# Hybrid decoder trunk on one core: the narrow projections' three products of 256 columns become one of 512 and one of 256

## The chip, the cores and the metric

One core of a Trainium2 chip runs the whole program. The time is device microseconds of one execution of the program, weights and activations being in the chip's own memory at the start.

## The reference

Two layers of one mixer each over 256 tokens of width 2048, then a last RMSNorm. All in float32.

```python
for l in range(DEPTH):
    h = rmsnorm(x, norm_w[l])
    proj = jnp.einsum('bld,dn->bln', h, w_in[l]).astype(f32)
    (gdn_qkv, gdn_b, gdn_a, gdn_z, hg_q, hg_f, hg_i, hg_g, s5_u, s5_z,
     ret_q, ret_k, ret_v, ret_g, gate_logits) = jnp.split(proj, split_idx, axis=-1)
    ...
    ys = jnp.stack([y_a, y_b, y_c, y_d], axis=2).astype(x.dtype)
    branch = jnp.einsum('blcw,cwd->blcd', ys, w_branch[l]).astype(f32)
    merged = jnp.sum(gates * branch, axis=2)
    x = x + jnp.einsum('bld,de->ble', merged.astype(x.dtype), w_out[l])
```

The four branches are a gated DeltaNet (short causal convolution on query, key and value, L2 norms of key and query, chunkwise inverse), HGRN2, an S5 state space scan and a RetNet retention with rotary positions; each has 8 heads or 8 slices of 128 channels.

## The kernel before

A layer has two parts. First come eight **units**, one for each head (u = 0 to 7; n counts them over both layers, 0 to 15). A unit projects h for its 128 channels of all branches and does the mixing of that head in all four branches. Then come the stages behind the units: gates, the GLU of S5, the branch products and the output projection.

**Precision.** Every weight is used as a high part (`w_hi`, the weight as fp32r) and a low part (`w_lo`, the rest), and so is h (`h_hi`, `h_lo`). A product is three passes of PE that add up in one bank: w_hi with h_hi, w_hi with h_lo, w_lo with h_hi (`three_pass`, L1794).

**Slots.** Weights come in slots of 512 KB, four buffers in turn (RING = 4). For each slot SyncE loads `raw_w`, ACT copies it to `w_hi` (`split_hi`, L651), DVE subtracts to get `w_lo` (`split_lo`, L1223), PE multiplies. For slots 6, 8, 10, 16, 18, 20 and 22 of a unit (DMA_LOW) half of the low part is made by ACT (L649) and a DMA of GpSimd, and DVE makes only the other half. A unit has 28 slots:

- 0 to 11 and 20 to 27: the ten **narrow** blocks, two slots each, in the order S5 input (SU), key (GK), query (GQ), forget gate (HF), HGRN query (HQ), value (GV); after the joint slots retention query (RQ), key (RK), gate (RG), and S5 gate (SZ). Weights are the stationary operand, h moves with 256 columns, output is channels by tokens in half a bank. Two banks, PJ[0] and PJ[1], are used in turn.
- 12 to 19: the **joint** slots, h stationary, 512 columns of weights moving, both PJ banks whole.

**Order.** The order on each engine is written out by hand, and every engine works strictly in its own order. `project(i)` on PE waits for the low part of slot i and, at a block's first slot, for `pj_read`, which tells that the bank's last block has been read; its last product counts `split_used`. On ACT and DVE `ahead(i)` makes the high or low part of slot i + 4. DVE's `ahead` waits for ACT's (`hi_ready`), ACT's for PE's end of slot i (`split_used`). Between these stand the steps of the mixing. ACT reads each narrow block out of its bank (`projected(b)` waits for PE's last slot of the block), in the form that it needs: `stage_conv` copies it for the convolution (L766) and scales it by the last tap (L767), `stage_rope` copies it and its swapped halves (L816 to L818), the others are one activation each (L829, L881, L897, L954, L962).

**The chain to the norms.** DVE's `conv_taps` (L1367) adds the other three taps, ACT's `silu_conv` applies SiLU (L776) and squares (L779), and PE's `g_norms`, behind slot 7, sums the squares of key and query (the product with `ones`, bank GB), followed by `g_gram_k` (bank S). DVE then makes the norm factors (`gnorm` L1518, GpSimd's power L585, `gfac` L1524), the masked Gram matrix, and with `invert` and PE's `g_tx`, `g_txt` the inverse level by level; `h_scores` (L1436 on) are the levels of HGRN2. `s5_turn` (L1402 to L1405), `s5_add` (L1411, L1412) and `s5_scan` (L1420) are the state space steps, `ret_finish` (L1344) and `rope` (L1462 to L1465) belong to retention. In the traces the buffers conv_in and gk, gq, gv read partly as mix and work, since names are shared; the rows give the lines.

Of the kernel before, what the change touches and what calls it, by code (L numbers as in the profile page):

```python
# [21 lines left out]
P = 128  # L22
D_MODEL, SEQ, DEPTH = 2048, 256, 2
# [23 lines left out]
(B_SU, B_GK, B_GQ, B_HF, B_HQ, B_GV, B_RQ, B_RK, B_RG, B_SZ) = range(10)  # L47

# [115 lines left out]
def trunk_kernel(nc, A, out):  # L164
# [4 lines left out]
    with ctx:  # L169
# [25 lines left out]
        h_hi, h_lo = sb("h_hi", [P, KT, SEQ], f32r), sb("h_lo", [P, KT, SEQ], f32r)  # L195
# [179 lines left out]
        pj_read = sem("pj_read")  # L375
# [16 lines left out]
        u_staged, s5_used = sem("u_staged"), sem("s5_used")  # L392
# [229 lines left out]
        def _(act):  # L622
# [30 lines left out]
            for l in range(DEPTH):  # L653
# [84 lines left out]
                for u in range(UNITS):  # L738
# [6 lines left out]
                    def projected(b):  # L745

                        act.wait_ge(split_used, s0 + (block_slot(b) + 2 + RING))
                        return PJ[b % 2][:, 0:SEQ]

# [13 lines left out]
                    def stage_conv(b, m):  # L763

                        src = projected(b)
                        A_(conv_in[m][:, CONV - 1:], src, ACT.Copy)  # L766
                        A_((gk, gq, gv)[m], src, ACT.Copy, scale=tap(m, CONV - 1)).then_inc(pj_read, 1)  # L767
# [45 lines left out]
                    def stage_rope(m, b):  # L813

                        src = projected(b)
                        A_(rx[m][:, :], src, ACT.Copy)  # L816
                        A_(rsw[m][0:64, :], src[64:128, :], ACT.Copy)
                        A_(rsw[m][64:128, :], src[0:64, :], ACT.Copy).then_inc(pj_read, 1)  # L818
                        act.drain().then_inc(rope_staged, 1)
# [6 lines left out]
                    def stage_u():  # L826

                        act.wait_ge(s5_used, n1)
                        A_(s_u[:, :], projected(B_SU), ACT.Copy).then_inc(pj_read, 1)  # L829
                        act.drain().then_inc(u_staged, 1)  # L830

                    ahead(0)
                    if u == 0:
                        stage_u()
# [26 lines left out]
                    else:  # L861
                        stage_bc()
                        delta_finish(u - 1)
                        stage_u()
# [16 lines left out]
                    A_(hsig[:, 0, :], projected(B_HF), ACT.Tanh, scale=0.5).then_inc(pj_read, 1)  # L881
# [15 lines left out]
                    A_(hq[:, :], projected(B_HQ), ACT.Silu).then_inc(pj_read, 1)  # L897
# [56 lines left out]
                    A_(gate_of(3), projected(B_RG), ACT.Silu).then_inc(pj_read, 1)  # L954
# [5 lines left out]
                    if u + 1 < UNITS:  # L960
                        cosines()
                    A_(zs[:, ds(u, 1), :].rearrange("p a n -> p (a n)"), projected(B_SZ), ACT.Silu).then_inc(  # L962
                        pj_read, 1)
# [398 lines left out]

# [967 lines left out]
```

## Time and profile before

| | |
|---|---|
| median of three runs | 2917.91 us (2917.57 to 2918.38) |
| the profiled execution | 2917.88 us, its span 2916.0 us |
| granted clock of TensorE, mean | 0.998 |
| PE, DVE, ACT, GpSimd busy | 98%, 68%, 54%, 14% |
| read from memory | 487 MB, 168 GB/s over the span |

The span is that from the first to the last instruction; about 1.9 us lie around it. PE is the matmul side of TensorE. Busy times of PE count products that overlap, so the rate at which it works is read from the starts of its instructions.

### The profile page before, as it was taken

What the parts mean: (1) busy time and instruction counts of PE and PEld (TensorE: products, weight loads), DVE (VectorE), ACT (ScalarE), POOL (GpSimd) and SP (SyncE); (2) the same over time, 40 slices, a digit from 0 to 9 for tenths busy, and PEclk for the clock granted to TensorE, in tenths of its full rate; (3) what the DMA queues carried; (4) which work ended last, traced back from release to release, by engine and by line L of the source; (5) the groups of instructions that cost most, each with busy time, mean ns of one, the idle gap of its engine ahead of it and who ended that gap; (6) DMA issues with size and microseconds to landing.
All of it is one profiled execution on the core that took longest, in us unless ns stands there. A gap on an engine that the chain in (4) does not pass through costs nothing.

```text
span 2916.0 us, 46745 instructions
## 1 busy us (share of the span) xinstructions
PE 2869.0 (98%) x17852; PEld 2562.9 (88%) x17852; DVE 1977.4 (68%) x3177; ACT 1574.0 (54%) x2401; POOL 422.3 (14%) x637
## 2 busy tenths in 40 slices
PE   7999999999999999999999999999999999999998
PEld 6899999999998888888889999999999888888887
DVE  6887788778875555555567877788778755555554
ACT  6556665666564444444556556655665644444443
POOL 3223132213200000000011332123211000000000
PEclk9999999999999999999999999999999999999999
DMA  6676677677766666666656766676667666666655
GB/s 163 163 172 166 175 181 174 164 177 179 175 175 195 194 194 195 193 192 185 192 129 165 178 171 174 172 179 171 171 171 181 181 195 195 192 192 195 194 180 166
DMA packets 636367, 521.56 MB, mean 179 GB/s; under 512 B 26480, under 2 KB 504496, under 8 KB 635760
## 3 DMA queue, kind: packets, MB, share of 16 engines
q1 hardware_dynamic: 612944, 483.46, 59.1%
q0 software_dynamic: 22816, 34.00, 6.8%
q8 instruction: 141, 2.31, 0.3%
q10 hardware_dynamic: 384, 1.11, 0.1%
q14 instruction: 82, 0.67, 0.1%
HBM read 487.02 MB, written 2.10 MB: 168 GB/s over the span
## 4 chain that ended last, share of the span: by engine, by line
PE 65%; issue 26%; DVE 4%; ACT 2%; DVEq 1%; POOL 1%; DMA 1%; ACTq 0%; POOLq 0%
PE PJ L1794 42%; PE S L1794 16%; PE RA L1794 3%; PE GB L1794 2%; DVE mix L1367 1%; DVE w_lo L1223 1%; POOL gnorm L585 0%; POOL w_lo L500 0%; DVE region L1402 0%; ACT w_lo L649 0%; DVE region L1404 0%; DVE region L1405 0%; DVEq L1406 0%; DVE region L1412 0%; DVEq L1413 0%
## 5 line engine op out<-in xcount | busy, mean ns | idle before, releaser
L1223 DVE TENSOR_TENSOR w_lo<-raw_w,w_hi 128x1024 fp32r<-128x1024 f32 (+1 forms) x912 | 1055.3, 1160 | 757.3 <-ACT w_hi L651 729.9
L651 ACT ACTIVATE w_hi<-raw_w 128x1024 fp32r<-128x1024 f32 x912 | 962.5, 1058 | 791.4 <-PE PJ L1794 342.5
L1794 PE MATMUL PJ<-h_hi,w_hi 128*128 128x256 f32 x2560 | 744.7, 291 | 1.6 <-DMA w_lo<-raw_w 1.6
L1794 PE MATMUL PJ<-h_hi,w_lo 128*128 128x256 f32 x2560 | 724.5, 283 | 0.0
L1794 PE MATMUL PJ<-h_lo,w_hi 128*128 128x256 f32 x2560 | 724.3, 283 | 0.0
L1794 PEld LDWEIGHTS PJ<-h_hi,w_hi 128*128 128x128 f32 x2560 | 490.4, 192 | 9.7 <-issue 6.8
L1794 PEld LDWEIGHTS PJ<-h_lo,w_hi 128*128 128x128 f32 x2560 | 490.6, 192 | 0.0
L1794 PEld LDWEIGHTS PJ<-h_hi,w_lo 128*128 128x128 f32 x2560 | 489.9, 191 | 0.0
L1794 PE MATMUL PJ<-w_hi,h_hi 128*128 128x512 f32 x1152 | 461.5, 401 | 1.9 <-DVE h_lo L1698 1.9
L1794 PE MATMUL PJ<-w_hi,h_lo 128*128 128x512 f32 x1152 | 450.4, 391 | 0.0
L1794 PE MATMUL PJ<-w_lo,h_hi 128*128 128x512 f32 x1152 | 449.9, 391 | 0.0
L1794 PEld LDWEIGHTS PJ<-w_hi,h_lo 128*128 128x128 f32 x1152 | 216.7, 188 | 46.6
L1794 PEld LDWEIGHTS PJ<-w_hi,h_hi 128*128 128x128 f32 x1152 | 217.2, 189 | 43.5 <-DVE h_lo L1698 2.4
L1794 PEld LDWEIGHTS PJ<-w_lo,h_hi 128*128 128x128 f32 x1152 | 217.1, 188 | 41.3
L1794 PE MATMUL S<-w_hi,h_hi 128*128 128x512 f32 x576 | 224.6, 390 | 0.0
L1794 PE MATMUL S<-w_hi,h_lo 128*128 128x512 f32 x576 | 224.2, 389 | 0.0
L1794 PE MATMUL S<-w_lo,h_hi 128*128 128x512 f32 x576 | 224.2, 389 | 0.0
L500 POOL DMA_DIRECT2D w_lo<-raw_w x112 | 99.0, 884 | 464.5 <-ACT w_lo L649 448.1
L795 ACT ACTIVATE work<-work 128x128 f32<-128x128 f32 x96 | 30.1, 313 | 201.7 <-PE S L1794 201.7
L1794 PEld LDWEIGHTS S<-w_hi,h_lo 128*128 128x128 f32 x576 | 108.1, 188 | 22.5
L1428 DVE TENSOR_TENSOR region<-region 128x1024 f32<-128x1024 f32 x96 | 117.6, 1225 | 15.1 <-issue 13.6
L1794 PEld LDWEIGHTS S<-w_lo,h_hi 128*128 128x128 f32 x576 | 108.2, 188 | 22.3
(386 smaller groups left out, 3988.6 us busy)
## 6 DMA issues: line engine op xcount, KB each, us to landing
raw_w<-w_in SPq DMA_DIRECT2D x576, 512.0 KB, 3.9
raw_w<-w_in SPq DMA_DIRECT2D x512, 128.0 KB, 2.7
raw_w<-w_branch SPq DMA_DIRECT2D x128, 512.0 KB, 4.2
raw_w<-w_out SPq DMA_DIRECT2D x64, 512.0 KB, 4.1
w_lo<-raw_w POOLq DMA_DIRECT2D x112, 256.0 KB, 4.3
raw_w<-s_glu_w SPq DMA_DIRECT2D x16, 512.0 KB, 4.5
ret_decay<-c_ret POOLq DMA_DIRECT2D x16, 128.0 KB, 3.8
out<-x_tok SPq DMA_DIRECT2D x4, 512.0 KB, 4.0
```

The lines of the kernel that those rows point to most:

```text
L500: pool.dma_start(w_lo[i % RING][:, OWN:, :], raw_w[i % RING][:, OWN:, :], accum_op=ALU.add).then_inc(low_landed, 16)
L651: A_(w_hi[i % RING][:, :, :], raw_w[i % RING][:, :, :], ACT.Copy).then_inc(hi_ready, 1)
L795: A_(blocks_of(rr[:, 1, :], 1 << s), in_turn(tt[:, 0, :], tt[:, 1, :], 1 << s), ACT.Copy)
L1223: TT(w_lo[i % RING][:, 0:ks, :], raw_w[i % RING][:, 0:ks, :], w_hi[i % RING][:, 0:ks, :].bitcast(f32), ALU.subtract).then_inc(raw_used[i % ...
L1367: last = STT(t, conv_in[m][:, k:k + SEQ], tap(m, k), t, ALU.mult, ALU.add)
L1428: TT(a, b, c, op)
L1794: return nc.tensor.matmul(o, w, m, start=start, stop=stop)
```

## The change

The high and low parts of h lie in one tensor, side by side for each k. A narrow step is one product of w_hi with both parts (512 columns, a whole bank) and one of w_lo with h_hi (256 columns, into the bank's first half). The bank then holds two halves that have to be added. A new DVE step, `sum_parts(b)`, does it with one TENSOR_REDUCE of 512 elements to 256, into the buffer where the block is wanted; it counts `pj_read`, and after a drain `summed`. ACT's steps wait for `summed` in place of PE and read SBUF; its first convolution copy, its first rope copy and `stage_u` are gone. The joint slots and the stages behind the units keep their products.

```diff
+NARROW = B_SZ + 1
...
-        h_hi, h_lo = sb("h_hi", [P, KT, SEQ], f32r), sb("h_lo", [P, KT, SEQ], f32r)
+        h_parts = sb("h_parts", [P, KT, 2, SEQ], f32r)
+        h_hi, h_lo = h_parts[:, :, 0, :], h_parts[:, :, 1, :]
...
                     def stage_conv(b, m):
 
-                        src = projected(b)
-                        A_(conv_in[m][:, CONV - 1:], src, ACT.Copy)
-                        A_((gk, gq, gv)[m], src, ACT.Copy, scale=tap(m, CONV - 1)).then_inc(pj_read, 1)
+                        act.wait_ge(summed, n * NARROW + (b + 1))
+                        A_((gk, gq, gv)[m], conv_in[m][:, CONV - 1:], ACT.Copy, scale=tap(m, CONV - 1))
...
                     def stage_rope(m, b):
 
-                        src = projected(b)
-                        A_(rx[m][:, :], src, ACT.Copy)
-                        A_(rsw[m][0:64, :], src[64:128, :], ACT.Copy)
-                        A_(rsw[m][64:128, :], src[0:64, :], ACT.Copy).then_inc(pj_read, 1)
+                        act.wait_ge(summed, n * NARROW + (b + 1))
+                        A_(rsw[m][0:64, :], rx[m][64:128, :], ACT.Copy)
+                        A_(rsw[m][64:128, :], rx[m][0:64, :], ACT.Copy)
...
-                    A_(hsig[:, 0, :], projected(B_HF), ACT.Tanh, scale=0.5).then_inc(pj_read, 1)
+                    act.wait_ge(summed, n * NARROW + (B_HF + 1))
+                    A_(hsig[:, 0, :], hsig[:, 0, :], ACT.Tanh, scale=0.5)
...
-                    A_(hq[:, :], projected(B_HQ), ACT.Silu).then_inc(pj_read, 1)
+                    act.wait_ge(summed, n * NARROW + (B_HQ + 1))
+                    A_(hq[:, :], hq[:, :], ACT.Silu)
...
+                    def sum_parts(b):
+
+                        dve.wait_ge(split_used, s0 + (block_slot(b) + 2 + RING))
+                        to = (s_u, conv_in[0][:, CONV - 1:], conv_in[1][:, CONV - 1:], hsig[:, 0, :], hq,
+                              conv_in[2][:, CONV - 1:], rx[0][:, :], rx[1][:, :], yT[:, 3, u, :], zs[:, u, :])[b]
+                        nc.vector.tensor_reduce(to, PJ[b % 2][:, :].rearrange("p (a n) -> p n a", a=2),
+                                                mybir.AxisListType.X, ALU.add).then_inc(pj_read, 1)
+                        dve.drain().then_inc(summed, 1)
...
                         ret_normalize(u - 1)
                         ahead(2)
                         s5_add(0)
+                        sum_parts(B_GK)
+                        ahead(3)
                         conv_taps(0)
-                        ahead(3)
                         ahead(4)
                         s5_turn(1)
-                        conv_taps(1)
+                        sum_parts(B_GQ)
                         ret_finish(u - 1)
                         ahead(5)
+                        conv_taps(1)
                         s5_add(1)
...
+                    dve.wait_ge(hgrn_used, n1)
+                    sum_parts(B_HF)
...
                         s5_scan(0)
+                        sum_parts(B_HQ)
                         ahead(9)
                         s5_scan(1)
                         invert(1)
 
+                        sum_parts(B_GV)
                         dve.wait_ge(hq_staged, n1)
                         h_scores(0)
...
                     s5_back(4)
+                    sum_parts(B_RQ)
                     ahead(21)
...
                     s5_back(5)
+                    sum_parts(B_RK)
                     ahead(23)
...
-                            last = three_pass(o[:, 0:SEQ], lambda k: (w_hi[i % RING][:, k, :], w_lo[i % RING][:, k, :]),
-                                              k, lambda k: (h_hi[:, h * HALF + k, :], h_lo[:, h * HALF + k, :]),
-                                              h == 0 and k == 0, h == 1 and k == HALF - 1)
+                            at = h * HALF + k
+                            MM(o[:, :], w_hi[i % RING][:, k, :], h_parts[:, at, :, :].rearrange("p a n -> p (a n)"),
+                               at == 0, False)
+                            last = MM(o[:, 0:SEQ], w_lo[i % RING][:, k, :], h_hi[:, at, :], False, at == KT - 1)
...
-                            pe.wait_ge(sa_r, sa0 + 3)
+                            pe.wait_ge(sa_r, sa0 + 4)
```

The other `sum_parts` stand at the same kind of place: SU behind `ahead(0)`, RG ahead of `ahead(25)`, SZ ahead of `ahead(27)`. In a layer's first unit GK, GQ, HQ and GV have their places in a similar way.

On DVE, unit 3 from the taps of the keys to the low part of slot 9, before:

```order
L1367 SCALAR_TENSOR_TENSOR mix<-conv_in,conv_w,mix 128x256 [waits conv_staged]
L1367 SCALAR_TENSOR_TENSOR mix<-conv_in,conv_w,mix 128x256 x2
L1223 TENSOR_TENSOR w_lo<-raw_w,w_hi 128x1024 [waits hi_ready]
L1223 TENSOR_TENSOR w_lo<-raw_w,w_hi 128x512 [waits hi_ready]
L1402 TENSOR_TENSOR region<-S,region 128x512 [waits sa_written]
L1403 TENSOR_TENSOR region<-S,region 128x512
L1404 TENSOR_TENSOR region<-S,region 128x512
L1405 TENSOR_TENSOR region<-S,region 128x512
L1367 SCALAR_TENSOR_TENSOR mix<-conv_in,conv_w,mix 128x256 [waits conv_staged]
L1367 SCALAR_TENSOR_TENSOR mix<-conv_in,conv_w,mix 128x256 x2
L1344 TENSOR_TENSOR y_all<-RA,y_all 128x256 [waits rz_staged,ra_written]
L1223 TENSOR_TENSOR w_lo<-raw_w,w_hi 128x1024 [waits hi_ready]
```

and now, from the sum of the keys:

```order
L1358 TENSOR_REDUCE conv_in<-PJ 128x256 [waits split_used]
L1213 TENSOR_TENSOR w_lo<-raw_w,w_hi 128x1024 [waits hi_ready]
L1366 SCALAR_TENSOR_TENSOR mix<-conv_in,conv_w,mix 128x256 [waits conv_staged]
L1366 SCALAR_TENSOR_TENSOR mix<-conv_in,conv_w,mix 128x256 x2
L1213 TENSOR_TENSOR w_lo<-raw_w,w_hi 128x512 [waits hi_ready]
L1401 TENSOR_TENSOR region<-S,region 128x512 [waits sa_written]
L1402 TENSOR_TENSOR region<-S,region 128x512
L1403 TENSOR_TENSOR region<-S,region 128x512
L1404 TENSOR_TENSOR region<-S,region 128x512
L1358 TENSOR_REDUCE conv_in<-PJ 128x256 [waits split_used]
L1334 TENSOR_TENSOR y_all<-RA,y_all 128x256 [waits rz_staged,ra_written]
L1213 TENSOR_TENSOR w_lo<-raw_w,w_hi 128x1024 [waits hi_ready]
```

The taps of the keys now stand behind the low part of slot 7, and those of the queries follow only behind the last row, the low part of slot 9.

On ACT, the same stretch, before:

```order
L766 ACTIVATE conv_in<-PJ 128x256 [waits split_used]
L767 ACTIVATE mix<-PJ,conv_w 128x256
L651 ACTIVATE w_hi<-raw_w 128x1024 [waits raw_full3,split_used]
L776 ACT_TABLE_LOAD
L776 ACTIVATE mix<-mix 128x256 [waits conv_summed]
L779 ACTIVATE work<-mix 128x256
```

and now:

```order
L763 ACTIVATE mix<-conv_in,conv_w 128x256 [waits summed]
L653 ACTIVATE w_hi<-raw_w 128x1024 [waits raw_full3,split_used]
L772 ACT_TABLE_LOAD
L772 ACTIVATE mix<-mix 128x256 [waits conv_summed]
L775 ACTIVATE work<-mix 128x256
```

The order is the same, but the first row waits for DVE's sum, and the high part of slot 7 stands behind it.

On DVE, later in the unit, from the first half of the S5 scan to the first product of HGRN2, now:

```order
L1419 SCALAR_TENSOR_TENSOR region<-s_par,region 128x256 x4
L1358 TENSOR_REDUCE hkq<-PJ 128x256 [waits split_used]
L1213 TENSOR_TENSOR w_lo<-raw_w,w_hi 128x1024 [waits hi_ready]
L1419 SCALAR_TENSOR_TENSOR region<-s_par,region 128x256 x4
L1378 TENSOR_TENSOR work<-am,masks 128x128
L1389 TENSOR_TENSOR work<-work,S 128x32x2x2 [waits ga_written]
L1389 TENSOR_TENSOR work<-work,S 128x32x2x2
L1358 TENSOR_REDUCE conv_in<-PJ 128x256 [waits split_used]
L1435 TENSOR_TENSOR hkq<-hkq,hf 128x256 [waits ha_written,hq_staged]
```

Before, it was the same without the two reduces, which are the HGRN query (ahead of the low part of slot 13) and the value.

## Rows read from the trace of the kernel before

**Rows 1.** The page, part 1: busy us, share of the span, instructions.
```profile
PE 2869.0 (98%) x17852; PEld 2562.9 (88%) x17852; DVE 1977.4 (68%) x3177; ACT 1574.0 (54%) x2401; POOL 422.3 (14%) x637
```

**Rows 2.** Windows, unit 3 and gates: stretch, length, busy us (instructions), clock, DMA share.
```profile
292.00:390.00 98.00, 97.86 (x740) 92.03 (x739) 78.09 (x151) 60.46 (x107) 26.44 (x38) 1.00 0.70 173
1250.00:1350.00 100.00, 100.00 (x443) 82.83 (x442) 50.75 (x46) 42.17 (x43) 0.00 (x0) 1.00 0.66 195
```

**Rows 3.** Waits: who waited for whom, us in total, times, longest.
```profile
DVE w_lo L1223 <- ACT w_hi L651: 729.9, 528, 5.3
```

**Rows 4.** Timeline of PE, unit 3: start us, us, instruction, tiles, form, count.
```profile
364.97 0.28 PE L1794 MATMUL PJ<-h_hi,w_lo 128*128 128x256 f32 x1
...
365.69 0.28 PE L1794 MATMUL PJ<-h_hi,w_lo 128*128 128x256 f32 x1
365.88 1.05 PE L1794 MATMUL GB<-ones,work 128*128 128x1 f32 x8
366.79 0.92 PE L1794 MATMUL S<-mix 128*128 128x128 f32 x6
```

**Rows 5.** Timeline of DVE, unit 3, slots 2 to 8.
```profile
350.64 0.69 DVE L1402 TENSOR_TENSOR region<-S,region 128x512 f32<-128x512 f32 x1 [1.14 <-PE S L1794]
...
355.28 0.68 DVE L1412 TENSOR_TENSOR region<-region 128x512 f32<-128x512 f32 x1
356.04 1.61 DVE L1367 SCALAR_TENSOR_TENSOR mix<-conv_in,conv_w,mix 128x256 f32<-128x256 f32 x3
...
363.27 1.61 DVE L1367 SCALAR_TENSOR_TENSOR mix<-conv_in,conv_w,mix 128x256 f32<-128x256 f32 x3
...
365.35 1.23 DVE L1223 TENSOR_TENSOR w_lo<-raw_w,w_hi 128x1024 fp32r<-128x1024 f32 x1
366.49 0.68 DVE L1411 TENSOR_TENSOR region<-region 128x512 f32<-128x512 f32 x1
...
367.85 0.16 DVE L1518 TENSOR_SCALAR gnorm<-GB 128x4 f32<-128x4 f32 x1
```

**Rows 6.** Timeline of ACT, unit 3, slots 3 to 8.
```profile
354.36 0.47 ACT L767 ACTIVATE mix<-PJ,conv_w 128x256 f32<-128x256 f32 x1
355.00 1.06 ACT L651 ACTIVATE w_hi<-raw_w 128x1024 fp32r<-128x1024 f32 x1 [0.17 <-issue]
...
364.91 0.42 ACT L776 ACTIVATE mix<-mix 128x256 f32<-128x256 f32 x1 [2.68 <-DVE mix L1367]
365.40 0.42 ACT L779 ACTIVATE work<-mix 128x256 f32<-128x256 f32 x1
...
367.19 0.36 ACT L881 ACTIVATE work<-PJ 128x256 f32<-128x256 f32 x1
...
368.90 1.06 ACT L651 ACTIVATE w_hi<-raw_w 128x1024 fp32r<-128x1024 f32 x1 [0.16 <-issue]
```

**Rows 7.** Timelines of DVE, ACT and PE, unit 3, around slot 12.
```profile
374.87 0.29 DVE L1550 COPY am<-S 128x128 f32<-128x128 f32 x1 [0.41 <-PE S L1966]
...
381.15 0.47 ACT L767 ACTIVATE mix<-PJ,conv_w 128x256 f32<-128x256 f32 x1
381.48 0.47 PE L1794 MATMUL PJ<-w_hi,h_hi 128*128 128x512 f32 x1
...
383.34 0.43 DVE L1436 TENSOR_TENSOR hkq<-hkq,hf 128x256 f32<-128x256 f32 x1 [0.19 <-issue]
```

**Rows 8.** Timelines of DVE and PE, unit 3, slots 22 to 26.
```profile
418.90 1.23 DVE L1223 TENSOR_TENSOR w_lo<-raw_w,w_hi 128x1024 fp32r<-128x1024 f32 x1 [1.73 <-ACT w_hi L651]
...
427.80 0.42 DVE L1465 TENSOR_TENSOR rx<-rx,rsw 128x256 f32<-128x256 f32 x1
428.61 0.82 PE L1794 MATMUL RA<-rx 128*128 128x256 f32 x4
```

**Rows 9.** Timeline of PE and windows, start of layer 2.
```profile
1468.31 0.94 PE L1794 MATMUL S<-am,x_tok 128*128 128x128 f32 x6 [2.98 <-DVEq L1218]
...
1468.00:1472.00 4.00, 3.69 (x21) 3.69 (x22) 2.33 (x5) 1.47 (x4) 0.00 (x0) 0.65 0.32 73
```

More of the change, by code:

```diff
@@ L374, in trunk_kernel @@
         g_ready, gc_written, cols_ready = sem("g_ready"), sem("gc_written"), sem("cols_ready")
-        pj_read = sem("pj_read")
+        pj_read, summed = sem("pj_read"), sem("summed")
         ga_w, ga_r = sem("ga_written"), sem("ga_read")
@@ L391, in trunk_kernel @@
         rope_staged, roped, ret_used = sem("rope_staged"), sem("roped"), sem("ret_used")
-        u_staged, s5_used = sem("u_staged"), sem("s5_used")
+        s5_used = sem("s5_used")
         phase_rounded, phase_ready, sincos_ready, x_re_im_ready = (
@@ L743, in _ @@
                     ha0, sa0, cv0 = n * HA_N, n * SA_N, n * 3
-                    def projected(b):
-                        act.wait_ge(split_used, s0 + (block_slot(b) + 2 + RING))
-                        return PJ[b % 2][:, 0:SEQ]
                     def ahead(i):
@@ L824, in stage_bc @@
                         A_(bc_T[:, :, :], SA, ACT.Copy).then_inc(sa_r, 1)
[L826 to L830, printed above, removed]
                     ahead(0)
                     if u == 0:
-                        stage_u()
                         ahead(1)
@@ L863, in _ @@
                         delta_finish(u - 1)
-                        stage_u()
                         ahead(1)
@@ L953, in _ @@
                     act.drain().then_inc(g_ms_ready, 1)
-                    A_(gate_of(3), projected(B_RG), ACT.Silu).then_inc(pj_read, 1)
+                    act.wait_ge(summed, n * NARROW + (B_RG + 1))
+                    A_(gate_of(3), gate_of(3), ACT.Silu)
                     act.drain().then_inc(rz_staged, 1)
@@ L961, in _ @@
                         cosines()
-                    A_(zs[:, ds(u, 1), :].rearrange("p a n -> p (a n)"), projected(B_SZ), ACT.Silu).then_inc(
-                        pj_read, 1)
+                    act.wait_ge(summed, n * NARROW + (B_SZ + 1))
+                    A_(zs[:, u, :], zs[:, u, :], ACT.Silu)
                     ahead(27)
@@ L1471, in _ @@
                             s5_ratio()
+                        sum_parts(B_SU)
                         ahead(1)
@@ L1488, in _ @@
                         ahead(4)
+                        sum_parts(B_GQ)
+                        ahead(5)
                         conv_taps(1)
-                        ahead(5)
                         if n:
@@ L1499, in _ @@
                         ahead(0)
+                        sum_parts(B_SU)
                         ahead(1)
@@ L1507, in _ @@
                         s5_add(0)
+                        sum_parts(B_GK)
+                        ahead(3)
                         conv_taps(0)
-                        ahead(3)
                         ahead(4)
                         s5_turn(1)
-                        conv_taps(1)
+                        sum_parts(B_GQ)
                         ret_finish(u - 1)
                         ahead(5)
+                        conv_taps(1)
                         s5_add(1)
@@ L1576, in _ @@
                             s5_turn(0)
+                            sum_parts(B_HQ)
                             ahead(9)
@@ L1579, in _ @@
                         else:
+                            sum_parts(B_HQ)
                             ahead(9)
@@ L1582, in _ @@
                         invert(1)
+                        sum_parts(B_GV)
                         dve.wait_ge(hq_staged, n1)
@@ L1654, in _ @@
                     dve.drain().then_inc(s5_used, 1)
+                    sum_parts(B_RG)
                     ahead(25)
@@ L1664, in _ @@
                     ahead(26)
+                    sum_parts(B_SZ)
                     ahead(27)
@@ L2022, in s_bu @@
                     def s_bu(half):
-                        pe.wait_ge(u_staged, n1)
+                        pe.wait_ge(summed, n * NARROW + 1)
                         pe.wait_ge(sa_r, sa0 + (2 + half))
@@ L2038, in s_bu_all @@
                     def s_bu_all():
-                        pe.wait_ge(u_staged, n1)
+                        pe.wait_ge(summed, n * NARROW + 1)
                         pe.wait_ge(sa_r, sa0 + 2)
```

## The prediction

> **What bounds the kernel now.** The page comes first: PE is busy 98% of the span, DVE 68%, ACT 54% [rows 1]. A busy PE need not be a PE at its limit, so the windows come next. In unit 3 (292 to 390 us, one of fourteen alike) PE is busy 97.9 of 98 us, DVE 78.1, ACT 60.5 [rows 2]. Third, the starts of PE's instructions: in the stream of 256 columns six starts take 0.72 us, so 120 ns each [rows 4]; in a stage of products of 512 columns 443 take 100 us, so 226 ns each [rows 2]. The length of a row (0.28 us for 256 columns [rows 4]) is a latency that overlaps the next and prices nothing. Length from start to start is columns at 2.4 GHz (107 and 213 ns) plus about 13 ns, and the granted clock is 1.00. PE is the bound: it hardly waits. But it hardly waits by a hair. Look at where slot 7 ends: the last of its products starts at 365.69, the norm sums of the delta branch start at 365.88 [rows 4], and what they wait for, the square of ACT, starts at 365.40 and lasts 0.42, so it ends at 365.82 [rows 6]. That side chain has no slack at all. DVE and ACT do wait for each other much of the time (729.9 us of DVE's idle time ends with ACT's high part [rows 3]), which is harmless only while both run some us ahead of PE.
>
> **The products.** Each k step of a narrow slot was three products of 256 columns, 3 x 120 = 360 ns; it is now one of 512 and one of 256, 226 + 120 = 346 ns. No column is saved, one handover of 13 to 14 ns is. 2,560 such steps (20 slots of 8, 16 units) give 36 us, or 2.24 us per unit. That is the whole gain on PE.
> By the Trainium skill (TensorE: Matmul & The Clock Gate, section on the back-to-back issue gap) the gap is N/2.4 + 2.5 ns, which would save only 2.5 ns per step, 6 us in all; it would put the sum 30 us higher. The rows measure the gap in this very stream, so the rows decide.
>
> **The sums.** Ten reduces per unit go to DVE. No such instruction is in the trace. Nearest is the multiply that reads 512 elements of a bank: 0.69 us, and 0.61 to 0.76 to the next one, the latter with a drain behind (355.28 to 356.04 [rows 5]). I take 0.76 with its drain; the lower bound is a 256 element operation, 0.42 long, the upper two passes over the bank, 1.3. Ten make 7.6 us per unit, and DVE had 20 idle. In bulk they fit. The cost is in the order, since each sum puts DVE into a chain that was ACT's alone, and ACT's splits of the next weights now queue behind the wait for the sum, and DVE's low parts behind those.
>
> **Place A, keys and queries to the norms.** Old chain in unit 3: scores of S5 at 350.64, taps of the keys at 356.04, SiLU and square on ACT, low part, turn, taps of the queries at 363.27, SiLU 364.91, square until 365.82, PE at 365.88 [rows 4 to 6]. New, ahead of the taps of the keys: sum 0.76, ACT's scaled copy with its drain 0.64 (354.36 to 355.00), the high part of slot 7 1.06 [rows 6], its low part on DVE 1.14 (365.35 to 366.49 [rows 5]): DVE's next row is that low part, and it needs ACT's high part, which sits behind the copy that needs the sum. Together 3.6 us. In the old order the same four stood beside the path. The queries repeat it: another 3.6 us, and 0.2 for handoffs; the retention product (0.56) hides beside ACT. The chain starts from PE (after slot 2), so its head moves with PE; PE itself arrives 5 slots x 0.11 = 0.56 earlier. PE waits 7.4 + 0.6 = 8.0 us for the norm sums, in each unit but the first of a layer.
>
> **Place B, the values before the joint slots.** The bank's second half is needed 1.35 us into slot 12, which starts at 381.48 [rows 7]; that second half is 16.95 after the norm sums began, now 16.5. ACT read the values at 381.15 to 381.62, 1.2 us before. DVE's road is longer: the norm factors begin at 367.85, the work up to the product of 383.34 takes 15.5 [rows 5, 7]. To it come three sums (forget gate, HGRN query, value) 2.3, less the 0.4 that DVE idled at 374.87 [rows 7]; a wait for the high part of slot 11, which stands behind the three gate activations of ACT (367.19 to 368.90, then 1.06 [rows 6]: 2.8 after the sum), while DVE has 1.9 of other work and idled 0.3 before, so 0.6; a wait for the high part of slot 13 behind the query's SiLU, 0.6 + 1.06, with nothing between, 1.7. Sum 19.7, and 1.1 from the first norm product to the factors: the value's sum ends 20.7 after them. PE waits 4.2 us there.
> From there to slot 20 nothing is added; DVE is late by as much as PE.
>
> **Place C, retention.** Rope of the key ends at 427.80 + 0.42, PE's scores start at 428.61 [rows 8]: slack 0.3. The query's sum pushes the high part of slot 25, on which DVE already idled until 418.90 [rows 8], by 1.1. The key's sum 0.76, two half-width copies with a drain 1.0, and the high part of slot 27, 1.06, stand newly in DVE's way: 2.8. PE arrives 0.7 earlier. 1.1 + 2.8 + 0.7 - 0.3 = 4.3 us of waiting, shared between the delta output and the retention scores.
> The other sums (S5 input, gates) fall on idle DVE time. Cover: about 0.8 us before the next unit's first S5 multiply; with a dearer reduce it is gone and place A grows.
>
> **Sum.** 8.0 + 4.2 + 4.3 - 2.2 = 14.3 per unit, and 0.5 for the clock (below); 14 units give 207. The first unit of each layer has other work between the same steps; I take 10 each, 20. The stages behind the units have no narrow projection and stay. 2917.9 (the profiled execution; its span is 2916.0, and the median of the three runs 2917.91, the same) + 227 = **3145 us**.
>
> **The clock.** After 2.98 us of idle PE at the start of layer 2 the granted clock is 0.65 in the next 4 us, that is, some 2.8 us of it at 1.2 GHz [rows 9]. Eight idle us at place A should bring that too, costing 1.7 to 3 us of PE. Most is hidden, since PE waits at B for a DVE chain that depends on PE only through the Gram products: 0.5 left.
> The same page of the Trainium skill, TensorE: Matmul & The Clock Gate, in its table on why this matters, advises against idle gaps between bursts for that reason; the rows of layer 2 agree.
>
> **Rivals.**
> 1. Cover holds: DVE's 20 idle us take sums and handoffs, and PE keeps its lead. Then only the products count, 2917.9 - 36 = 2882. It decides at place A: if the square still ends before slot 7 does. For it: the low part of slot 9 begins at 365.35 [rows 5], before slot 8 is even started, so splits as such have room. Against: zero slack at A and two round trips of 3.6 added. 4%.
> 2. Only A bites; the time PE loses there lets DVE catch up, and B and C vanish: (8.0 - 2.2) x 16 = 93, 3010. Against: B's and C's chains begin from events that A delays as well. 16%.
> 3. Dearer: a reduce of 1.3 us (two more in A, three in B, two in C, 0.5 each, 3.5), a clock fall after C not hidden, 1.7, and a mixed pair that gains nothing because handover from 512 to 256 columns is slower, 2.2: 7.4 x 16 = 118 more, 3263. That the products don't do what they say is this last part alone, 3181. 14%.
> Mine: 66%, with 3080 to 3200 as its own range.
>
> **How the numbers follow.** The range takes in rival 2 and half of rival 3: 3005 to 3245, with about 2 in 10 outside. A change of 0.2% (6 us) can be told from none. Faster 4% (rival 1), same 1%, slower 95%.
>
> **What would show it.** PE idle of about 8 us per unit ahead of the norm sums, released by ACT's square; about 4 in slot 12 at its second half, released by DVE's reduce (and partly at the transposed inverse before it, by ACT); about 4 before the delta output and the retention scores. The reduce near 0.65 us. DVE's idle time ended by ACT's high part grows, ACT's ended by a reduce is new. Products of 512 columns at 226 ns, of 256 at 120. A unit some 14 us longer, the stages behind unchanged. Wrong would be: a PE share still at 98%, or a reduce far from 0.7, or waits at A below 5 us.

## The result, and the profile after

| | before | changed |
|---|---|---|
| median | 2917.94 us (2917.57 to 2918.38, 4 runs) | 3204.93 us (3201.70 to 3208.96, 4 runs) |
| ratio, 95% interval | | 1.0984 [1.0965, 1.1003] |
| span of the profiled execution | 2916.0 us | 3207.1 us |
| granted clock of TensorE, mean | 0.998 | 0.956 |
| one unit (norm sums to norm sums, mean of twelve) | 97.6 us | 116.7 us |

The kernel is 287 us slower. Fourteen units with 19.2 more each are 269 of it. The rest is known as a difference alone (18 us by the medians, 22 by the two spans): some 9 to 11 us for the first unit of each layer.

The page of the changed kernel, part 1, and three groups of its part 5 (busy us and mean ns, then the idle time ahead of them with what ended it):

```profile
PE 2960.5 (92%) x15292; PEld 2494.9 (78%) x15292; DVE 2084.0 (65%) x3337; ACT 1543.5 (48%) x2305; POOL 395.1 (12%) x637
...
L1810 PE MATMUL PJ<-w_hi,h_parts 128*128 128x512 f32 x2304 | 766.8, 403 | 33.7 <-DVE conv_in L1358 31.8
...
L1810 PE MATMUL GB<-ones,work 128*128 128x1 f32 x128 | 28.2, 342 | 106.3 <-ACT work L775 106.3
...
L763 ACT ACTIVATE mix<-conv_in,conv_w 128x256 f32<-128x256 f32 x48 | 24.5, 510 | 201.3 <-DVEq L1360 201.3
```

Against [rows 1] no engine is fuller: each has a smaller share of a longer span. What is new stands at the right. The norm sums (place A), with 3.0 us of idle time ahead of them before, have 106 us of waiting for ACT's square; the joint slots (place B) 32 for the sum of the values; and ACT's scaled copy waits 201 us for the drain behind a sum (L1360). The share of PE hides how much this is: its idle time grew from 47 us (2916.0 less 2869.0) to 247 (3207.1 less 2960.5). The waits view puts a count to each (total, times, longest):

```profile
DVE w_lo L1213 <- ACT w_hi L653: 842.1, 599, 5.3
...
ACT mix L763 <- DVEq L1360: 201.3, 48, 5.2
...
PE GB L1810 <- ACT work L775: 106.3, 15, 7.9
...
PE S L1810 <- DVEq L1658: 41.1, 16, 2.9
...
PE PJ L1810 <- DVE conv_in L1358: 31.8, 14, 2.4
```

DVE's idle time ended by the high part grew from 729.9 [rows 3] to 842.1. L1658 is DVE's copy for the delta output: place C. Now unit 3 at place A, PE's timeline (start, length, instruction, [idle before <- releaser]):

```profile
413.10 0.28 PE L1810 MATMUL PJ<-h_parts,w_lo 128*128 128x256 f32 x1
413.22 0.40 PE L1810 MATMUL PJ<-h_parts,w_hi 128*128 128x512 f32 x1
413.45 0.28 PE L1810 MATMUL PJ<-h_parts,w_lo 128*128 128x256 f32 x1
...
418.75 0.28 PE L1810 MATMUL PJ<-h_parts,w_lo 128*128 128x256 f32 x1
426.45 1.87 PE L1810 MATMUL GB<-ones,work 128*128 128x1 f32 x8 [7.42 <-ACT work L775]
428.18 1.63 PE L1810 MATMUL S<-mix 128*128 128x128 f32 x6
```

In [rows 4] 0.19 us lay between the last product's start and the norm sums; here 7.70, of which 0.12 is the product's own time: a wait of 7.6. And the norm sums take 1.87 where they took 1.05. DVE and ACT in the same stretch show the two round trips:

```profile
408.54 0.69 DVE L1411 TENSOR_TENSOR region<-region 128x512 f32<-128x512 f32 x1
409.30 0.69 DVE L1358 TENSOR_REDUCE conv_in<-PJ 128x256 f32<-128x512 f32 x1
411.83 1.23 DVE L1213 TENSOR_TENSOR w_lo<-raw_w,w_hi 128x1024 fp32r<-128x1024 f32 x1 [1.84 <-ACT w_hi L653]
412.97 1.60 DVE L1366 SCALAR_TENSOR_TENSOR mix<-conv_in,conv_w,mix 128x256 f32<-128x256 f32 x3
417.01 0.69 DVE L1213 TENSOR_TENSOR w_lo<-raw_w,w_hi 128x512 fp32r<-128x512 f32 x1 [2.44 <-ACT w_hi L653]
...
420.19 0.69 DVE L1358 TENSOR_REDUCE conv_in<-PJ 128x256 f32<-128x512 f32 x1
...
422.71 1.22 DVE L1213 TENSOR_TENSOR w_lo<-raw_w,w_hi 128x1024 fp32r<-128x1024 f32 x1 [1.20 <-ACT w_hi L653]
423.86 1.61 DVE L1366 SCALAR_TENSOR_TENSOR mix<-conv_in,conv_w,mix 128x256 f32<-128x256 f32 x3
```

```profile
410.07 0.51 ACT L763 ACTIVATE mix<-conv_in,conv_w 128x256 f32<-128x256 f32 x1 [5.21 <-DVEq L1360]
410.73 1.06 ACT L653 ACTIVATE w_hi<-raw_w 128x1024 fp32r<-128x1024 f32 x1 [0.15 <-PE PJ L1810]
...
425.50 0.42 ACT L772 ACTIVATE mix<-mix 128x256 f32<-128x256 f32 x1 [2.82 <-DVE mix L1366]
425.99 0.42 ACT L775 ACTIVATE work<-mix 128x256 f32<-128x256 f32 x1
```

Read the first trip across the two: sum of the keys 409.30, its drain lets ACT start the scaled copy at 410.07 (0.77 later, after 5.21 idle), the high part follows at 410.73, the low part at 411.83, and only then the taps, 412.97. That is 3.67 us from sum to taps, the work of four instructions. The queries repeat it from 420.19 to 423.86, again 3.67. The reduce lasts 0.69.

The clock (windows of the changed kernel: stretch, length, busy us of PE, weight load, DVE, ACT and GpSimd, granted clock, DMA):

```profile
418.00:420.00 2.00, 1.03 (x6) 0.61 (x4) 2.00 (x4) 0.00 (x0) 0.00 (x0) 1.00 0.76 131
...
422.00:424.00 2.00, 0.00 (x0) 0.00 (x0) 1.29 (x2) 0.68 (x1) 0.00 (x0) 0.50 0.64 152
...
427.00:431.00 4.00, 4.00 (x18) 3.81 (x18) 2.21 (x8) 1.73 (x3) 2.35 (x4) 0.50 0.14 38
446.00:452.00 6.00, 3.56 (x12) 2.92 (x12) 4.58 (x10) 1.71 (x3) 0.51 (x1) 0.72 0.26 70
499.00:503.00 4.00, 3.82 (x22) 2.16 (x23) 2.78 (x4) 1.99 (x6) 1.76 (x2) 0.57 0.49 136
1400.00:1500.00 100.00, 100.00 (x443) 82.81 (x442) 51.05 (x45) 41.95 (x43) 0.00 (x0) 1.00 0.66 194
```

The clock falls to its lower level (1.2 GHz) during the wait at A, and is still there 4 us after PE is back. It falls again behind B and behind C. Over the whole run the mean granted clock of 0.956 means some 283 us at 1.2 GHz; the kernel before had 15. The last row is a stage behind the units: 443 products in 100 us, as in [rows 2]; nothing changed there.

Places B and C on PE's timeline:

```profile
443.51 0.71 PE L1810 MATMUL S<-work 128*128 128x128 f32 x4 [0.60 <-ACT work L792]
...
445.67 0.40 PE L1810 MATMUL PJ<-w_hi,h_parts 128*128 128x512 f32 x1
448.50 0.80 PE L1810 MATMUL PJ<-w_hi,h_parts 128*128 128x512 f32 x1 [2.44 <-DVE conv_in L1358]
...
494.98 0.28 PE L1810 MATMUL PJ<-h_parts,w_lo 128*128 128x256 f32 x1
497.80 0.94 PE L1810 MATMUL S<-work 128*128 128x128 f32 x6 [2.54 <-DVEq L1658]
499.18 1.43 PE L1810 MATMUL RA<-rx 128*128 128x256 f32 x4 [0.45 <-DVEq L1660]
500.54 1.96 PE L1810 MATMUL S<-region,bc_T 128*32 128x256 f32 x16
502.43 0.69 PE L1810 MATMUL PJ<-h_parts,w_hi 128*128 128x512 f32 x1
```

At B the bank's second half waits 2.6 us (2.83 less a product's 0.23) for the sum of the values; 0.8 went just before at the inverse (443.51), released by ACT, counted from the start of the product before it. At C 2.7 and 0.6. From 497.80 to slot 26 pass 4.6 us, for which the kernel before took 2.4.

### The profile page after: what moved, and what is told of

It is laid out like the page before. It is cut to its first block, busy times and chain, and to the rows that moved or that the text cites. A ratio compares the mean times of both kernels' runs of the same rounds, so it can differ in the third digit from the quotient of the medians.

```text
span 3207.1 us, 41833 instructions
## 1 busy us (share of the span) xinstructions
PE 2960.5 (92%) x15292; PEld 2494.9 (78%) x15292; DVE 2084.0 (65%) x3337; ACT 1543.5 (48%) x2305; POOL 395.1 (12%) x637
## 4 chain that ended last, share of the span: by engine, by line
PE 50%; issue 22%; DVE 14%; ACT 7%; DVEq 5%; ACTq 1%; DMA 1%; POOL 0%; POOLq 0%
PE PJ L1810 30%; PE S L1810 14%; DVE w_lo L1213 5%; ACT w_hi L653 4%; PE RA L1810 3%; PE GB L1810 2%; DVEq L1360 2%; DVE region L1427 1%; DVE region L1419 1%; DVE conv_in L1358 1%; DVE mix L1366 1%; DVE region L1404 1%; DVEq L1405 1%; DVE region L1403 1%; DVEq L1647 1%
## 5 line engine op out<-in xcount | busy, mean ns | idle before, releaser
L1213 DVE TENSOR_TENSOR w_lo<-raw_w,w_hi 128x1024 fp32r<-128x1024 f32 (+1 forms) x912 | 1054.9, 1160 | 863.5 <-ACT w_hi L653 842.1
L1810 PE MATMUL PJ<-h_parts,w_hi 128*128 128x512 f32 x2560 | 958.6, 414 | 0.1
L1810 PE MATMUL PJ<-w_hi,h_parts 128*128 128x512 f32 x2304 | 766.8, 403 | 33.7 <-DVE conv_in L1358 31.8
L1810 PE MATMUL PJ<-h_parts,w_lo 128*128 128x256 f32 x2560 | 728.2, 284 | 0.0
L1810 PEld LDWEIGHTS PJ<-h_parts,w_hi 128*128 128x128 f32 x2560 | 497.1, 194 | 121.0 <-issue 11.2
L1810 PEld LDWEIGHTS PJ<-w_hi,h_parts 128*128 128x128 f32 x2304 | 441.9, 192 | 130.0 <-DVE conv_in L1358 38.0
L1810 PEld LDWEIGHTS PJ<-h_parts,w_lo 128*128 128x128 f32 x2560 | 498.3, 195 | 0.0
L1810 PE MATMUL PJ<-w_lo,h_parts 128*128 128x512 f32 x1152 | 456.8, 397 | 0.0
L1810 PE MATMUL S<-w_hi,h_parts 128*128 128x512 f32 x1152 | 368.9, 390 | 0.3 <-DVE w_lo L1213 0.2
L1810 PEld LDWEIGHTS PJ<-w_lo,h_parts 128*128 128x128 f32 x1152 | 221.3, 192 | 41.7
L1810 PE MATMUL S<-w_lo,h_parts 128*128 128x512 f32 x576 | 224.1, 389 | 0.0
```

The costliest lines, as they stand in the source:

```text
L1213: TT(w_lo[i % RING][:, 0:ks, :], raw_w[i % RING][:, 0:ks, :], w_hi[i % RING][:, 0:ks, :].bitcast(f32), ALU.subtract).then_inc(raw_used[i % ...
L1810: return nc.tensor.matmul(o, w, m, start=start, stop=stop)
```

## The experiments

Two theories. Mine: the loss lies in the order; sums that stand inside the ACT and DVE chain make waits at A, B and C, and the clock adds to them. Rivals: the load that the sums put on DVE, or the new products themselves.

**Run 1, the products alone.** The kernel before with the new products; ACT goes on reading the bank's first half, so the product of w_hi with h_lo is left out of the result.

```diff
-                            last = three_pass(o[:, 0:SEQ], lambda k: (w_hi[i % RING][:, k, :], w_lo[i % RING][:, k, :]),
-                                              k, lambda k: (h_hi[:, h * HALF + k, :], h_lo[:, h * HALF + k, :]),
-                                              h == 0 and k == 0, h == 1 and k == HALF - 1)
+                            at = h * HALF + k
+                            MM(o[:, :], w_hi[i % RING][:, k, :], h_parts[:, at, :, :].rearrange("p a n -> p (a n)"),
+                               at == 0, False)
+                            last = MM(o[:, 0:SEQ], w_lo[i % RING][:, k, :], h_hi[:, at, :], False, at == KT - 1)
```

> The kernel before with the new narrow products alone: ACT still reads the blocks out of the bank, and only the bank's first half, so the product of w_hi with h_lo is left out of the result; there is no sum on DVE and no wait on it. Theory 1 (the changed kernel's rows: a pair takes 350 ns against 360): 2,560 steps save about 9 ns each, 22 us, and nothing stands in their way: 2896 us. Theory 2 (the edges without slack, places A and C, give it back): PE arrives earlier at chains of ACT and DVE that end no earlier, and most of the 1.4 us per unit turns into waits: 2905 to 2912. The prediction's own price (14 ns) would give 2882.

Measured: 2908.22 us, ratio 0.9963 [0.9949, 0.9977]: some 10 us faster; the mean unit takes 96.7 us, 0.8 less. The median step is 350 ns. The mean of about 2,060 undisturbed steps is 351 against 359 before, so 8 ns a step, 1.3 us a unit and 21 us in all; 11 of them come back as small waits of PE. The largest that the trace shows is at the norm sums: from the last product of slot 7 to their start it takes 9.5 us over the sixteen units, 6.2 before. Smaller ones stand at the retention products; the rest was not traced. At the norm sums it looks like this (PE, then ACT):

```profile
365.36 0.28 PE L1795 MATMUL PJ<-h_parts,w_lo 128*128 128x256 f32 x1
365.75 1.05 PE L1795 MATMUL GB<-ones,work 128*128 128x1 f32 x8
```

```profile
365.27 0.42 ACT L780 ACTIVATE work<-mix 128x256 f32<-128x256 f32 x1
```

The square ends at 365.69 and PE goes on at 365.75. A place with no slack keeps a faster PE from being a faster kernel.

**Run 2, the sums alone.** The changed kernel with the three old products in the bank's first half; the reduce reads that half twice, so the narrow blocks come out doubled.

```diff
-                        nc.vector.tensor_reduce(to, PJ[b % 2][:, :].rearrange("p (a n) -> p n a", a=2),
+                        nc.vector.tensor_reduce(to, PJ[b % 2][:, 0:SEQ].unsqueeze(2).to_broadcast([P, SEQ, 2]),
```

> The changed kernel with the three old products of 256 columns in the bank's first half, and every reduce, drain, wait and order on DVE and ACT kept; the reduce reads the first half twice, so the narrow blocks come out doubled. If the whole loss is the order (theory 1), the time stays that of the changed kernel, 3200 to 3225 us, since what PE loses on products it waits less. If products of 512 columns or the full bank had a part in it (rival), the time falls clearly, below 3150.

Measured: 3210.30 us, ratio 1.1004 [1.0982, 1.1026], 5 us more than the changed kernel. The new products have no part in the loss.

**Run 3, the clock at A.** The changed kernel; in all but first units PE does 20 products into a free bank, whose result nobody reads, while it would wait for the norm sums.

```diff
+                    if n % UNITS:
+                        pe.wait_ge(pj_read, pj0 + 5)
+                        for _ in range(20):
+                            MM(PJ[0][:, :], h_parts[:, 0, 0, 0:P], h_parts[:, 0, :, :].rearrange("p a n -> p (a n)"))
                     g_norms()
```

> The changed kernel with 20 added products of 512 columns (4.5 us, result thrown away) in the free bank ahead of the norm sums in 14 units, where PE idles 7.6 us; they fit in the wait and keep PE at work. Theory 1 (the granted clock costs 2.2 us at place A, which my prediction put at 0.5): the clock stays at 1.00 behind A, and a unit gains 1.5 to 2.5 us, 3170 to 3184 us in all. Rival (the clock's loss is hidden behind the wait at place B, as predicted): a gain under 0.7 us per unit, 3195 to 3205.

Measured: 3175.93 us, ratio 1.0886 [1.0864, 1.0908]; clock 0.975. The 29 us over 14 units make 2.1 us a unit. PE's timeline shows why, in unit 2 and in unit 3:

```profile
300.23 4.81 PE L1810 MATMUL PJ<-h_parts 128*128 128x512 f32 x20 [1.89 <-DVE conv_in L1358]
...
414.58 6.41 PE L1810 MATMUL PJ<-h_parts 128*128 128x512 f32 x20 [1.90 <-DVE conv_in L1358]
420.83 0.94 PE L1810 MATMUL GB<-ones,work 128*128 128x1 f32 x8
```

In seven units the twenty take 4.8 us, near the 20 x 0.226 = 4.5 of 2.4 GHz. In the other seven they take 6.4: there the clock fell after the 1.9 us of waiting, part of them pays for it in place of the kernel's own work, and the norm sums start some 0.7 us later than they could. So 2.1 is the least that the clock costs at A. Work that serves nothing makes this kernel faster. The Trainium skill (TensorE: Matmul & The Clock Gate, its table on why this matters) advises against idle gaps between bursts; this run gives that advice its price here, and the price at A is at least a tenth of the loss.

**Runs 4, 5 and 6: the order mended at A, at C, and at A, B and C.** Only DVE's order changes; work, counts and engines stay (B's part is shown at run 7). A:

```diff
                         ahead(2)
-                        s5_add(0)
                         sum_parts(B_GK)
-                        ahead(3)
+                        s5_add(0)
                         conv_taps(0)
+                        ahead(3)
+                        sum_parts(B_GQ)
                         ahead(4)
                         s5_turn(1)
-                        sum_parts(B_GQ)
+                        conv_taps(1)
                         ret_finish(u - 1)
                         ahead(5)
-                        conv_taps(1)
```

The two steps of S5, and the low part of slot 8, now fill the time in which ACT makes its copies, and the taps stand ahead of the low parts of slots 7 and 9 again. C does the same in retention:

```diff
-                    s5_back(4)
                     sum_parts(B_RQ)
+                    s5_back(4)
                     ahead(21)
...
-                    s5_back(5)
                     sum_parts(B_RK)
-                    ahead(23)
+                    s5_back(5)
...
                     dve.drain().then_inc(roped, 1)
+                    ahead(23)
```

> The changed kernel with place A's order mended on DVE alone: the sum of the keys ahead of the S5 add, their taps ahead of the low part of slot 7, the sum of the queries ahead of the low part of slot 8, their taps ahead of retention's product and the low part of slot 9. ACT's copy and high parts then run beside DVE's other work. Theory 1: the wait for the norm sums falls from 7.6 to about 1.3 us, the clock does not fall there (2.2), and place B's wait grows by about 3 since its chain was partly hidden: 5 to 6 us less per unit, 3120 to 3140 us. Rival (DVE's added 7.6 us per unit are the bound, wherever they stand): the wait moves to place B whole, and the time stays above 3180.

> The changed kernel with place C's order mended on DVE alone: the sum of the retention query ahead of a multiply of S5, the sum of the key ahead of the last one, and the copy that the delta output needs and the rope of the key ahead of the low part of slot 27. Theory 1 (place C costs what the changed kernel's rows show, about 5 us per unit, waits and clock): 4 us less in each of 16 units, 3130 to 3150 us. Rival (DVE and ACT enter the next unit no earlier, so that the time comes back at place A): above 3180.

> The changed kernel with all three places mended on DVE: A and C as in the two runs of one place, and at B the sum of the forget gate ahead of the low part of slot 10, that of the HGRN query ahead of the first S5 scans, that of the value ahead of the second. Theory 1 (the loss is the order): most of it goes; the 1.5 us per unit that DVE's saturated stretch (slots 10 to 19) still has to take, and 1 us at C remain: 2960 to 3010 us. Rival (DVE's added work is the bound there): above 3040.

Measured: A alone 3090.23 us, ratio 1.0592 [1.0571, 1.0614] (115 us back, 8.2 in each of 14 units), C alone 3140.64, ratio 1.0761 [1.0740, 1.0783] (64, or 4.0 in each of 16 units, since all have place C), all three 2975.90, ratio 1.0197 [1.0180, 1.0214], clock 0.990. A gave more than expected, since B's wait did not grow in return: in the waits view of A alone it stands at

```profile
PE PJ L1810 <- DVE conv_in L1358: 33.8, 14, 2.5
```

against 31.8. That fits a chain to the values that starts from events which A delays too, so that it moves with A. Place A of that kernel:

```profile
397.64 0.28 PE L1810 MATMUL PJ<-h_parts,w_lo 128*128 128x256 f32 x1
398.89 1.05 PE L1810 MATMUL GB<-ones,work 128*128 128x1 f32 x8 [0.97 <-ACT work L775]
```

The wait is 1.1 us where it was 7.6. DVE does the same work in all these kernels, so the load of the sums as such is not the bulk of the loss.

**Run 7, B alone**, for the part that run 6 leaves unnamed: the sums of forget gate and query each ahead of what stood before them, that of the values ahead of the second half of the scan.

```diff
+                    dve.wait_ge(hgrn_used, n1)
+                    sum_parts(B_HF)
                     if u:
                         ahead(6)
 
-                    dve.wait_ge(hgrn_used, n1)
-                    sum_parts(B_HF)
...
+                        sum_parts(B_HQ)
                         s5_scan(0)
-                        sum_parts(B_HQ)
                         ahead(9)
+                        sum_parts(B_GV)
                         s5_scan(1)
                         invert(1)
 
-                        sum_parts(B_GV)
```

> The changed kernel with place B alone mended, as in the run of all three. Theory 1: the wait for the value's sum (2.6 us), the one for ACT's copy before it (0.8) and the clock after them (1.4) go, and a wait of about 2 us for the first HGRN2 level takes their place, since DVE carries three sums more by then: 2.5 us less per unit, 3160 to 3180 us. Rival (the wait only moves to the next edge): above 3195.

Measured: 3163.68 us, ratio 1.0840 [1.0819, 1.0862]: 41 us back. The three alone give 115, 41 and 64, together 220; in one kernel 229. They nearly add up, so none hides behind another to speak of.

**Run 8, for the 58 us left.** Run 6, and more of DVE's work moved out of the first half of the unit. The lines are against the changed kernel, so the sums of run 7 are in them again:

```diff
+                        sum_parts(B_HQ)
+                        s5_add(1)
                         s5_scan(0)
-                        sum_parts(B_HQ)
                         ahead(9)
-                        s5_scan(1)
+                        sum_parts(B_GV)
...
                         h_scores(3)
                         ahead(13)
+                        scan_one(1)
```

`scan_one` is one of the four scans of `s5_scan(1)`. Two of them now stand one by one behind the low parts of slots 16 and 17, the other two together behind that of slot 18. The second S5 add stands behind the norm factors, the second taps precede the second turn, the retention statistics precede the low part of slot 5, and in a layer's first unit too the taps stand ahead of the low parts.

> The kernel with all three places mended (2975.9 us), and DVE's order changed where its rows still show PE waiting: the variance of retention ahead of the low part of slot 5 and its product ahead of the first S5 multiplies (0.9 us), the taps of the queries ahead of the second S5 multiplies (1.1), the second S5 add behind the norm factors (0.9), the second four scans taken apart and put where DVE waited for PE in the HGRN2 levels (2.1); in a layer's first unit the taps ahead of the low parts. Theory 1 (the loss was order all along): 3.5 to 5 us less per unit, 2905 to 2925 us; the floor is 2908, the time with the products alone. Rival (DVE's stretch of slots 8 to 19 has no room for three sums): the scans push the HGRN2 levels back, and the time stays above 2945.

Measured: 2956.46 us, ratio 1.0131 [1.0114, 1.0148]. The rival had it: 19 us, not 50 to 70. PE at the norm sums of that kernel:

```profile
376.51 0.28 PE L1819 MATMUL PJ<-h_parts,w_lo 128*128 128x256 f32 x1
377.36 1.05 PE L1819 MATMUL GB<-ones,work 128*128 128x1 f32 x8 [0.57 <-ACT work L775]
378.91 1.62 PE L1819 MATMUL S<-mix 128*128 128x128 f32 x6 [0.50 <-DVE region L1404]
```

The norm sums come sooner (0.7 us of wait, 1.1 in run 6), but in unit 3 the turn that the Gram products wait for comes later, and the clock falls there. What moved ahead of one wait moved behind the next. The windows give a likely reason: the 39 us from slot 3 to slot 12 of the kernel before, and 40 us in the same place of run 6:

```profile
347.00:366.00 19.00, 19.00 (x164) 18.22 (x163) 15.56 (x29) 12.08 (x20) 3.25 (x4) 1.00 0.55 131
366.00:386.00 20.00, 19.86 (x148) 18.89 (x149) 18.12 (x37) 10.72 (x19) 14.32 (x23) 1.00 0.72 171
```

```profile
361.00:381.00 20.00, 19.02 (x118) 15.72 (x117) 17.95 (x33) 12.45 (x19) 3.18 (x4) 1.00 0.65 166
381.00:401.00 20.00, 18.14 (x107) 15.55 (x107) 17.78 (x35) 9.85 (x16) 13.48 (x23) 1.00 0.72 178
```

DVE was busy 33.7 of 39 us there already, 5.3 idle, and five of the ten sums with their drains, 3.8 us, fall in it. The 20 idle us of [rows 2] lie mostly in the rest of the unit. That this shortage holds the last 39 us of run 8 is argued from these rows; no run took load away in this stretch alone, and DVE is not full there in run 6 either, it idles 4.3 us of the 40.

Where the 58 us of run 6 sit can be read, though. PE's idle time is 101 us (2974.1 less the 2873.4 of its page) against 47, so 54 more. In a unit it waits 1.1 us at the norm sums, 0.8 behind the first HGRN2 level and 0.6 for DVE's use of the retention output. The time at 1.2 GHz is 59 us against 15; the 44 more cost at most half, 22. The products give some 20 back. So what is left is again waits at chains of DVE and ACT, with the clock on top.

**Run 9, only sums outside that stretch.** The kernel before, with new products and sums for S5 input, retention gate and S5 gate alone.

```diff
+SUMMED = (B_SU, B_RG, B_SZ)
...
+                            if b in SUMMED:
+                                at = h * HALF + k
+                                MM(o[:, :], w_hi[i % RING][:, k, :], h_parts[:, at, :, :].rearrange("p a n -> p (a n)"),
+                                   at == 0, False)
+                                last = MM(o[:, 0:SEQ], w_lo[i % RING][:, k, :], h_hi[:, at, :], False, at == KT - 1)
+                                continue
```

> The kernel before, with the new products and a sum on VectorE only in the three blocks that the prediction called free (S5 input, retention gate, S5 gate); the other seven blocks keep three products of 256 columns and are read by ScalarE. Theory 1 (these sums fall on idle VectorE time, nothing of them reaches PE): the products save at most 0.3 of the 22 us that the pairs save in the changed kernel, 7 us, and by the share that reached the end in the run with the products alone (10 of 22) 3 us: 2911 to 2917, and the wait at the norm sums stays near 0.2 us. Theory 2 (each sum also makes VectorE late for the low parts behind it, and the S5 chain up to the taps of the keys passes that on to the norm sums, which had no slack): 1.1 to 1.4 us more per unit at the norm sums after the S5 input's sum, 2930 to 2945.

Measured: 2915.83 us against 2917.16 for the kernel before beside it, ratio 0.9993 [0.9984, 1.0002]. Three sums a unit cost nothing that shows, as theory 1 has it; what the products save in six slots of 28 is too little to tell from none. The groups of instructions have, for the retention gate and the S5 gate (busy us, mean ns, idle before):

```profile
L1363 DVE TENSOR_REDUCE y_all<-PJ 128x256 f32<-128x512 f32 x32 | 22.0, 687 | 2.2
```

DVE hardly waits ahead of them. ACT waits 54 us over the run for their drains, which is off the path: PE's idle time ahead of the norm sums is 2.9 us over the whole run, 3.0 in the kernel before. It is the only version without a part left out that is not slower than before.

## Why the prediction was right, and where its sizes were off

The forecast was 3145, the time is 3205: inside the range, 5 us above the 3080 to 3200 that the prediction gave to its own mechanism. The mechanism is the one forecast: runs 1 and 2 put the whole loss on the sums and their order, and undoing the order at the three named places brings 229 of 287 us back. The sizes miss on both sides, and part of that cancels: the waits were put 1.9 us a unit too high, the clock 4.2 too low, the gain of the products 0.9 too high. Step by step, in us per unit:

| step | forecast | measured |
|---|---|---|
| products | -2.24 | -1.3 (8 ns x 160 steps, run 1) |
| one reduce with its drain | 0.76 | 0.77 (409.30 to 410.07) |
| A: one round trip | 3.6 | 3.67 and 3.67 |
| A: wait at the norm sums | 8.0 | 7.6 |
| B: waits | 4.2 | 0.8 + 2.6 |
| C: waits | 4.3 | 0.3 + 2.7 + 0.6 |
| clock | 0.5 | 2.1 or more (A, run 3), some 1.2 (B) and 1.4 (C) by the starts in unit 3 |
| first unit of a layer | 10 | 9 to 11, by difference |
| stages behind the units | 0 | 0 (443 products in 100 us) |

- **The products** failed as a size. The step "226 + 120 = 346" added two pitches, each from a stream of its own kind. In the mixed stream the pair takes 350 (413.10 to 413.45), with a mean of 351, and the steps before had a mean of 359, not 360. 21 us in place of 36. The gap of the Trainium skill (TensorE: Matmul & The Clock Gate, section on the back-to-back issue gap), 2.5 ns for each product, would have given 6; the section gives it for a product by itself, not for a stream in which every product has its own weight load, as here. The trace stands between the two: 768 columns at 2.4 GHz are 320 ns, so a mixed pair has 15 ns of handover for each of its two products, where the three of 256 columns had 13 each.
- **The clock** is the step that was wrong in kind: "Most is hidden". Its price at A was worked out well (1.7 to 3; run 3 gives at least 2.1), but nothing hid it, and B and C have falls of their own, for waits of no more than 2.7 us, which the sum left out and only rival 3 had in part. The argument was that PE waits at B for a DVE chain that hardly depends on PE. It does depend: the chain to the values starts from the norm sums and the Gram products, which ran at half clock themselves. Behind B and C no wait stood to cover anything.
- **The waits** came to 14.6, against 16.5. Waits, clock and products make 14.6 + 4.7 - 1.3 = 18.0 of the 19.2. The last 1.2 was not traced to one place; most of it may be clock, since PE worked 12.6 us a unit at 1.2 GHz, and the half of that, 6.3, is the most that it can cost.
- **Of the rivals**, the first falls with place A, the second too: B and C did not vanish when A was there, and their gains add up. Of the third, the clock behind C is true, the dear reduce is not (0.69 us), and of the pair's gain some 6 of 14 ns are lost, not all.
- **The other sums** were said to hide in idle DVE time. Run 9 bears that out.
- What the prediction did not see is the second layer of the loss. It read DVE's 20 idle us of 98 as room for all ten sums "in bulk" and put the whole cost on order. Order was 229 us; with it mended 58 stay against the kernel before, 68 against run 1, which has the same products without sums. That the stretch between slots 3 and 12 had no such room is the likely reason, argued and not shown.

## What to carry to other kernels

Before a step is moved from one in-order engine to another, write down what already stands behind it there: here a 0.7 us sum cost 3.7 us each time, since ACT's copy, its next high part and DVE's low part had to follow it in turn before DVE could go on, and moving the same sums by a few rows brought back four fifths of the loss. Read idle time in the stretch in which the new work must run, not over the whole period (5 of 39 us here, not 20 of 98; run 9, whose sums stand outside it, cost nothing that shows). Gains on the bounding engine count only where no side chain is just as long: run 1 kept 10 of 21 us. And where waits are short but many, read the granted clock behind each: here it adds about a third to what the waits cost.

## What the runs showed of the hardware

- **The mixed pair.** From a product of 512 columns to the next start 233 ns, from one of 256 columns 117 (medians), where streams of one kind have 226 and 120: the handover depends on which shape follows.
- **The clock.** In unit 3 it stood at 1.2 GHz from about 421 to 431 us, though PE was busy again from 426.45; with PE waiting 7.6 us that cost at least 2.1 us a unit (run 3). Waits of 2.6 to 2.7 us at B and C were followed by some 3.4 us at 1.2 GHz each. In run 6 the wait of 1.1 us at the norm sums had no fall behind it in unit 3, where the two windows above read 1.00, and the same wait had one in unit 6 (norm sums at 683.6), so the length of the wait alone does not tell whether the clock falls:

```profile
686.00:688.00 2.00, 2.00 (x8) 1.71 (x8) 1.70 (x6) 1.18 (x3) 2.00 (x3) 0.50 0.80 209
```
- **The reduce.** 512 to 256 elements out of a bank, read with the two halves as the inner axis, lasts 0.69 us, no longer than an addition of 512 elements (0.69 at 408.54). The Trainium skill (VectorE: DVE Perf Modes, rules for kernel authors) calls this operation the slowest of DVE and advises to restructure. In float32 from a bank it was not slower than its neighbours here; its place in the order was the cost.
